# Products spread over four steps, latent heads in pairs, side steps after the third tile, and 768 tokens as 384 and 384

## The chip, the cores and the metric

The kernel runs on one core of a Trainium2 chip, as one launch. The metric is the time of the launch in microseconds on the device, as the median of several runs. TensorE (PE) multiplies; its weight loads (PEld) are told apart in the profile. VectorE (DVE), ScalarE (ACT) and GpSimd (POOL) do the element-wise work, SyncE (SP) starts most transfers. Lines such as L822 are lines of the kernel before.

## The reference

Two transformer blocks of two layers each are run one after the other on 512 tokens of 1024 features, all in float32. In layer 0 of the first block 256 context tokens run along, so that its linears see 768 tokens. Cut to what the change touches:

```python
# first block, layer 0 (with context): dense attention; layer 1: a band of 128 tokens plus the context, with a sink logit
p = jax.nn.softmax(s, axis=-1).astype(v.dtype)
o = jnp.einsum('bkgqt,btkd->bqkgd', p, v)
h = modulate(x, g_pre_mix[l], sh_m, sc_m); hc = modulate(ctx, g_pre_mix[l], csh_m, csc_m)
x = x + gt_f * rmsnorm(swiglu(h, w_ffn_in[l], w_ffn_out[l]), g_post_ffn[l])     # and the same for ctx in layer 0

# second block, layer 0: eight heads share one latent of 128 features and one rope key of 32
qc = jnp.concatenate([q_lat, q_rope], axis=-1)
kc = jnp.concatenate([c_kv, k_rope], axis=-1)
_, idx = lax.top_k(score, k_sel)                     # 128 tokens are kept of those up to the query
s = jnp.einsum('bqhc,bqkc->bqhk', qslice(qc, i, Q_BLOCK), kg).astype(jnp.float32) * A_SCALE
p = safe_softmax(s, valid)
return jnp.einsum('bqhk,bqkc->bqhc', p.astype(kg.dtype), kg[..., :A_KV_RANK])
```

## The kernel before

The features lie on the partitions and the tokens along the free axis. Each step of the network is a stage (a class derived from `Stage`); every engine has its own program, written out stage by stage, and the engines meet through semaphores. No scheduler moves anything: the order on each engine is that of the code.

**Linears** (`Linear`, the PE line L822, and L800 for the first two tiles of a linear whose input is still being made). A linear goes by output tiles of 128 features, called slabs. A slab's weights come in float32, ACT copies them to `w_hi` (L638), POOL subtracts to `w_lo` (L760), and PE multiplies hi by hi, hi by lo and lo by hi for each chunk of 128 input features. PE waits for `w_hi`, for `w_lo` before the last third, and for `psum_free`, the sign that DVE has emptied the two PSUM banks of the slab two before. The tokens are cut into groups, `self.groups`, and each group is a matmul with a weight load of its own. At 768 tokens the groups are 512 and 256 (258 where two columns of shift sums ride along). With `halves`, which only the shifted linears of 512 tokens have, they are 256 and 258. In the first block's layer 0 some linears also have `ModRows` beside them: DVE sums rows of the modulation weights (L389) in the same loop.

**Side steps** (`RopeBeside` and its children `WindowBeside`, `LatentBeside`, `CompressBeside`). While a linear runs, its finished tiles are rotated: PE multiplies a tile by a rotation matrix (L1095), POOL multiplies by the cosine (L1104), DVE does the sine and the sum (L1123, L1125). `beside.tensor(pe, m)` is called after slab m's matmuls and works on tile m - 1, for which it waits on `tile_out`. The first two slabs are done together by `two`, and steps 0 and 1 are called right behind it.

**Attention** (`Attend`). A unit is one head and 128 queries: scores on PE (L2499, the masks L2501), the row maximum on DVE (L1711), the exponential on ACT (L1768), the transposes of the probabilities on PE in two parts (L1666 into bank 4, L1671 into bank 5), copied out by DVE (L1742) and ACT (L1781). Four units are a batch with one output bank; B batches make a turn. `steps` sets one unit at each step and, Z + 1 steps later, part of the batch before. With `spread=True` (layer 0, its context, and the two window stages of layer 1) the batch's products are 4 that spread 1/sum over the columns (L2509) and 4 to 12 with the values (L2513), each onto 64 of the 128 output partitions; all of them are issued at the batch's step 0. ACT copies the spread columns at step 3 (L1795) and DVE multiplies at step 4 (L2520). The latent heads of the second block use `Attend` too, without `spread`: 16 batches of two units, J = 2.

`PairAttend` is the other form: two heads in one round, their scores in two PSUM banks, one `tensor_reduce` for both. The differential heads use it with `one` (the two heads are summed before the transposes) and the last attention without.

Of the kernel before, what the change touches and what calls it, by code (L numbers as in the profile page):

```python
# [522 lines left out]
class Linear(Stage):  # L523
# [7 lines left out]
    def __init__(self, kit, w, hi, lo, groups, mode, dst=None, segs=None, side=None, rows=None, norm=None, post=None, tiles=None, close=False, latent=()):  # L531
# [10 lines left out]
        self.halves = self.shifted and self.T == SEQ  # L542
        self.groups = [(0, SEQ // 2), (SEQ // 2, SEQ + 2)] if self.halves else ([(0, SEQ), (SEQ + 2, TOK + 4)] if norm.twice else [(0, SEQ), (SEQ, TOK + 2)]) if self.shifted else groups
# [23 lines left out]
    def main(self, s):  # L567

        k = self.kit
        return k.ps[:, 2 * s:2 * s + 2, 0:SEQ // 2] if self.halves else flat(k.ps[:, self.step * s:self.step * s + self.step])[:, :self.T]  # L570
# [9 lines left out]
    def shift_sums(self, s):  # L580
        return self.kit.ps[:, 2 * s + 1, SEQ // 2:SEQ // 2 + 2]
# [63 lines left out]
    def empty(self, eng, scale, m, e):  # L645
# [3 lines left out]
        tokens = self.tokens  # L649
        if self.norm:  # L650
            r = k.n_r[:, :T].unsqueeze(1)
# [5 lines left out]
            ins = eng.scalar_tensor_tensor(two(dst[:, 0, :]) if tokens is not self.tokens else dst, src, scale, r, ALU.mult, ALU.mult)  # L657
# [16 lines left out]
        if self.mode == "add":  # L674
            ins = eng.tensor_tensor(dst, src, dst, ALU.add)  # L675
        elif scale != 1.0:
            ins = eng.tensor_scalar(dst, src, scale, None, ALU.mult)
        else:
            ins = eng.tensor_copy(dst, src)
# [125 lines left out]
    def tensor(self, pe):  # L805
        k = self.kit

        def tile(m, i, e, parts=None, wait=lambda part, c: None):
# [35 lines left out]
        if isinstance(a, (Modulation, Gate)):  # L844
# [8 lines left out]
            if self.beside:  # L853
                for m in range(2):
                    self.beside.tensor(pe, m)
            self.slabs(pe, tile, 2)
            return
        if a and a.post:
# [10 lines left out]
            if self.beside:  # L869
                for m in range(2):  # L870
                    self.beside.tensor(pe, m)
            self.slabs(pe, tile, 2)
            return
        if a and a.mode == "gated":
# [6 lines left out]
            if self.beside:  # L881
                for m in range(2):
                    self.beside.tensor(pe, m)
# [648 lines left out]
class Attend(Stage):  # L1532
# [115 lines left out]
    def tensor(self, pe):  # L1648
# [32 lines left out]
        def output(j, n, i):  # L1681
# [120 lines left out]
class PairAttend(Stage):  # L1802
# [8 lines left out]
    def __init__(self, kit, J, scores, pv, prepare, finish, pt, one, adds=None):  # L1811
        super().__init__(kit)
        self.J, self.N, self.B, self.scores, self.pv, self.prepare, self.finish, self.pt, self.one, self.adds = J, J * QT, J * 2, scores, pv, prepare, finish, pt, one, adds
# [3 lines left out]
            ("pv_ready", self.B), ("spread_ready", 0 if one else self.B), ("o_free", self.B),  # L1817
# [28 lines left out]
    def tensor(self, pe):  # L1846
# [5 lines left out]
        def turn_round(p):  # L1852
            nt = p % QT + 1
            if self.one:
                pe.wait_ge(*self.count("prepared", p + 1))
                if p >= 2:
                    pe.wait_ge(*self.count("pt_b", p - 1))
# [7 lines left out]
        def output(b):  # L1865
            pe.wait_ge(*self.count("pt_b", 2 * b + 2))
            if not self.one:
                pe.wait_ge(*self.count("pt_a", 2 * b + 2))
                pe.wait_ge(*self.count("prepared", 2 * b + 2))
# [15 lines left out]
    def vector(self, dve, chain):  # L1885
# [6 lines left out]
        def take(b):  # L1892
            dve.wait_ge(*self.count("pv_ready" if self.one else "spread_ready", b + 1))
# [22 lines left out]
    def scalar(self, act, chain):  # L1916
# [15 lines left out]
        for p in range(self.N):  # L1932
            if p + 1 < self.N:
                exp(p + 1)
            if not self.one and p >= 3 and p % 2 == 1:
# [3 lines left out]
        if not self.one:  # L1939
# [517 lines left out]
def plan(k, d):  # L2457
# [172 lines left out]
    def scores_latent(pe, s, j, a, qi):  # L2630
        rows, n, q = slice(32 * a, 32 * a + 32), (qi + 1) * P, slice(qi * P, (qi + 1) * P)
        pe.matmul(s[:, 0:n], k.qlat[:, 4 * j + a, q], k.ckv_s[:, 0:n], start=True, stop=False, skip_group_check=True)  # L2632
# [318 lines left out]
```

## Time and profile before

| | |
|---|---|
| median of three runs | 3372.45 us (3364.27 to 3375.6) |
| the profiled execution | 3378.23 us, span 3376.4 us |
| mean granted TensorE clock | 0.943 |
| PE busy | 3076.1 us (91%), 16970 matmuls |
| DVE, ACT, POOL busy | 51%, 33%, 31% |
| HBM | 253.03 MB read, 76 GB/s over the span |

The page counts an engine as busy from an instruction's start to its end, and a matmul's end is modelled, so that two matmuls in a row overlap and a busy PE may still be waiting. What one matmul costs is read from starts: a row of the chain of waits gives the time of a run of matmuls and their number.

### The profile page before, as it was taken

How to read it: one execution, taken by the hardware profiler on the slowest of the kernel's cores; microseconds unless marked ns; L12 is line 12 of the kernel's file. 1: busy time of each engine (PE TensorE's matmuls, PEld its weight loads, DVE VectorE, ACT ScalarE, POOL GpSimd, SP SyncE). 2: the span in 40 equal slices, each digit the busy share in tenths (PEclk: the TensorE clock that was granted, in tenths of full speed). 3: DMA queues.
4: the chain of work that ended last, by engine and by line, in shares of the span. 5: the costliest groups of instructions: out<-in, count | busy, mean ns of one | idle time of the engine just before them, and what ended most of it. 6: DMA issues, size and time to landing. Idle time of an engine off the chain costs nothing.

```text
span 3376.4 us, 48629 instructions
## 1 busy us (share of the span) xinstructions
PE 3076.1 (91%) x16970; PEld 2493.5 (74%) x16970; DVE 1709.3 (51%) x2892; ACT 1101.2 (33%) x1904; POOL 1052.0 (31%) x573
## 2 busy tenths in 40 slices
PE   6778779999997888899998999899999999899997
PEld 3666668888886766699895765688887866688886
DVE  4755768864335566433245766342333247643433
ACT  3145143111124255432224324352223226552222
POOL 1121122323322311244443420244444301244443
PEclk8889989999998899899999988899999969999998
DMA  6200413434211100222222210222223100022222
GB/s 238 77 1 8 142 63 127 171 124 137 75 50 45 43 1 33 67 89 93 94 84 69 75 38 1 80 98 93 93 93 118 55 15 2 14 97 96 93 94 81
DMA packets 74344, 258.83 MB, mean 77 GB/s; under 512 B 9456, under 2 KB 12016, under 8 KB 72688
## 3 DMA queue, kind: packets, MB, share of 16 engines
q1 hardware_dynamic: 60256, 205.61, 18.4%
q10 hardware_dynamic: 13968, 51.65, 4.5%
q8 instruction: 73, 1.20, 0.1%
q14 instruction: 47, 0.39, 0.0%
HBM read 253.03 MB, written 2.10 MB: 76 GB/s over the span
## 4 chain that ended last, share of the span: by engine, by line
PE 81%; DVE 6%; issue 6%; ACT 3%; DVEq 1%; SPq 1%; ACTq 1%; POOL 0%; DMA 0%; POOLq 0%; PEldq 0%
PE ps L822 56%; PE ps L800 6%; PE ps L2513 2%; PE ps L2499 2%; PE ps L2656 1%; PE ps L426 1%; PE ps L1862 1%; PE ps L1095 1%; DVE ps L389 1%; PE ps L2720 1%; PE ps L1666 1%; DVE nm L1711 1%; ACT w_hi L638 1%; PE ps L2633 1%; PE ps L2632 1%
## 5 line engine op out<-in xcount | busy, mean ns | idle before, releaser
L760 POOL TENSOR_TENSOR w_lo<-w_raw,w_hi 128x1024 fp32r<-128x1024 f32 (+1 forms) x373 | 919.6, 2468 | 1823.5 <-ACT w_hi L638 1823.5
L638 ACT ACTIVATE w_hi<-w_raw 128x1024 fp32r<-128x1024 f32 (+1 forms) x373 | 385.6, 1038 | 1192.3 <-PE ps L822 948.0
L822 PE MATMUL ps<-h_hi,w_hi 128*128 128x258 f32 (+2 forms) x1824 | 315.6, 326 | 50.1 <-ACT w_hi L638 46.1
L822 PEld LDWEIGHTS ps<-h_hi,w_hi 128*128 128x128 f32 x1824 | 268.4, 195 | 85.6 <-issue 45.1
L822 PE MATMUL ps<-h_lo,w_hi 128*128 128x258 f32 (+2 forms) x1824 | 299.7, 316 | 0.0
L822 PE MATMUL ps<-h_hi,w_lo 128*128 128x258 f32 (+2 forms) x1824 | 296.7, 314 | 0.0
L822 PEld LDWEIGHTS ps<-h_lo,w_hi 128*128 128x128 f32 x1824 | 260.2, 190 | 24.4 <-DVE h_lo L2275 0.4
L822 PEld LDWEIGHTS ps<-h_hi,w_lo 128*128 128x128 f32 x1824 | 258.4, 189 | 23.1
L918 DVE CAST act_hi<-f_t 128x512 f32 (+1 forms) x88 | 165.8, 1884 | 12.6
L822 PE MATMUL ps<-hb_hi,w_hi 128*128 128x512 f32 x672 | 166.7, 390 | 2.0 <-issue 1.7
L822 PE MATMUL ps<-hb_hi,w_lo 128*128 128x512 f32 x672 | 166.0, 389 | 0.0
L822 PE MATMUL ps<-hb_lo,w_hi 128*128 128x512 f32 x672 | 166.0, 389 | 0.0
L822 PE MATMUL ps<-act_hi,w_hi 128*128 128x512 f32 (+1 forms) x660 | 151.6, 375 | 13.4 <-ACT w_hi L638 13.0
L822 PE MATMUL ps<-act_lo,w_hi 128*128 128x512 f32 (+1 forms) x660 | 149.4, 371 | 0.0
L822 PE MATMUL ps<-act_hi,w_lo 128*128 128x512 f32 (+1 forms) x660 | 148.6, 370 | 0.0
L822 PEld LDWEIGHTS ps<-hb_hi,w_hi 128*128 128x128 f32 x672 | 125.7, 188 | 30.4 <-issue 4.5
L822 PEld LDWEIGHTS ps<-hb_lo,w_hi 128*128 128x128 f32 x672 | 126.1, 188 | 26.2
L822 PEld LDWEIGHTS ps<-hb_hi,w_lo 128*128 128x128 f32 x672 | 126.1, 188 | 26.2
L1711 DVE TENSOR_REDUCE nm<-ps 128x1 f32<-128x512 f32 (+5 forms) x144 | 100.7, 700 | 88.2 <-PE ps L2501 45.7
L822 PEld LDWEIGHTS ps<-act_hi,w_hi 128*128 128x128 f32 x660 | 115.2, 190 | 40.7 <-issue 11.0
L675 DVE TENSOR_TENSOR x<-ps,x 128x512 f32 x64 | 44.3, 692 | 196.1 <-PE ps L822 166.1
L822 PE MATMUL ps<-ha_hi,w_hi 128*128 128x512 f32 x472 | 135.5, 431 | 8.9 <-ACT w_hi L638 7.9
(345 smaller groups left out, 5179.9 us busy)
## 6 DMA issues: line engine op xcount, KB each, us to landing
w_raw<-in_ffn_in SPq DMA_DIRECT2D x176, 512.0 KB, 3.4
mod_row<-in_w_mod_rows ACTq DMA_DIRECT2D x80, 512.0 KB, 4.3
w_raw<-in_ffn_out SPq DMA_DIRECT2D x64, 512.0 KB, 3.4
w_raw<-in_ev_in SPq DMA_DIRECT2D x26, 512.0 KB, 3.5
w_raw<-in_ffn_out SPq DMA_DIRECT2D x32, 384.0 KB, 3.0
w_raw<-in_od_in SPq DMA_DIRECT2D x21, 512.0 KB, 3.4
mod_ring<-in_w_mod SPq DMA_DIRECT2D x8, 1024.0 KB, 13.2
w_raw<-in_wo_in SPq DMA_DIRECT2D x12, 512.0 KB, 3.5
```

Of the source, the lines that this page charges most:

```text
L389: dve.scalar_tensor_tensor(flat(k.ps[:, 6:8]), k.mod_row[:, s, q], 1.0, (k.c_x, k.c_c)[j][:], ALU.mult, ALU.mult, accum_out=k.modv[:, tile ...
L426: ins = pe.matmul(k.ps[:, bank + g, 0:t1 - t0], k.ones[:], squares[:, t0:t1], start=start, stop=stop, skip_group_check=True)
L638: act.activation(k.w_hi[:, s, 0:self.KT * P], k.w_raw[:, s, 0:self.KT * P], ACT.Copy).then_inc(k.sems["w_hi_ready"], 1)
L675: ins = eng.tensor_tensor(dst, src, dst, ALU.add)
L760: ins = pool.tensor_tensor(k.w_lo[:, s, 0:self.KT * P], k.w_raw[:, s, 0:self.KT * P], k.w_hi[:, s, 0:self.KT * P].bitcast(F32), ALU.subtract)
L800: ins = pe.matmul(k.ps[:, self.step * s + g, 0:t1 - t0], w[:, s, c * P:(c + 1) * P], h[:, c, t0:t1], start=(e not in begun), stop=(left[e] ...
L822: ins = pe.matmul(k.ps[:, self.step * s + g, 0:t1 - t0], w[:, s, c * P:(c + 1) * P], h[:, c, t0:t1], start=(n == 0), stop=(n == len(parts) ...
L918: chain.mark(dve.tensor_copy(k.act_hi[:, at, :T], k.f_t[:, :T].unsqueeze(1)))
L1095: pe.matmul(self.bank(n), self.tiles[n].get("rot", self.rot), self.src(n), start=True, stop=True).then_inc(self.kit.sems["rot_mm"], 1)
L1711: ins = dve.tensor_reduce(k.nm[:, u % 4, 0:1], self.sc(u, n), AX.X, ALU.max, negate=True)
L2499: ins = pe.matmul(s[:, c:c + width], k.qs[:, a, q0:q0 + P], keys[:, part, t0:t0 + width], start=(part == 0), stop=(part == 1 and not masks ...
L2513: return made + [lambda i=i, a=a, slot=slot, t=t, c0=c0, c1=c1: pe.matmul(o[64 * a:64 * a + 64, c0:c1], v(a, t), pt[:, n % 2, a, slot, c0: ...
```

## The change

Four edits are made at once.

1. `Attend.output` loses its case for `spread`: a batch's products are issued in four parts at steps 0 to 3 (4, 4, 4, 4 in layer 0; 2, 2, 2, 2 for its context; 2, 4, 4, 4 in the windows), and `pv_ready` comes with the last part.
2. The latent heads go to `PairAttend`, two heads a round and 16 rounds in place of 32 units. `PairAttend` gets `spread` as an argument of its own, apart from `one`.
3. Side steps 0, 1 and 2 all follow slab 2.
4. `halves` also holds for linears of 768 tokens, except the one whose norm has `twice` (`wo_in`): groups 384 and 384, or 384 and 386 with the shift columns. These are `we_in`, `we_out`, and the six linears of the first feed-forward network.

```diff
+        self.half = self.T // 2
+        self.halves = self.shifted and self.T == SEQ or self.T == TOK and not (self.shifted and norm.twice)
+        self.groups = [(0, self.half), (self.half, self.T + 2 * self.shifted)] if self.halves else [(0, SEQ), (SEQ + 2, TOK + 4)] if self.shifted else groups
...
+        return k.ps[:, 2 * s:2 * s + 2, 0:self.half] if self.halves else flat(k.ps[:, self.step * s:self.step * s + self.step])[:, :self.T]
...
             if self.beside:
-                self.beside.tensor(pe, m)
+                for step in (range(3) if m == 2 else [m]):
+                    self.beside.tensor(pe, step)
...
             self.two(pe, order)
-            if self.beside:
-                for m in range(2):
-                    self.beside.tensor(pe, m)
             self.slabs(pe, tile, 2)
...
-            if self.spread:
-                part = lambda i: len(products) if i else 0
-            else:
-                part = lambda i: len(products) * i // self.Z // 2 * 2 if i < self.Z else len(products)
+            part = lambda i: len(products) * i // self.Z // 2 * 2 if i < self.Z else len(products)
             for product in products[part(i):part(i + 1)]:
                 ins = product()
-            if i == (0 if self.spread else self.Z - 1):
+            if i == self.Z - 1:
                 ins.then_inc(S["pv_ready"], 1)
...
+    turns2 = [(j, half) for j in range(2) for half in range(2)]
+
+    def scores_latent(pe, s, turn, qi):
+        j, half = turns2[turn]
+        n, q = (qi + 1) * P, slice(qi * P, (qi + 1) * P)
+        for a in range(2):
+            pe.matmul(s[:, a, :], k.qlat[:, 4 * j + 2 * half + a, q], k.ckv_s[:, 0:n], start=True, stop=False, skip_group_check=True)
+        for a in range(2):
+            at = 32 * (2 * half + a)
+            rows = slice(at, at + 32)
+            pe.matmul(s[:, a, :], k.qkv2[rows, 12 + j, q], k.qkv2[rows, 1, 0:n], start=False, stop=False, skip_group_check=True, tile_position=(at, 0))
+        for a in range(2):
+            ins = pe.matmul(s[:, a, :], k.ident_b, k.chosen[:, qi, 0:n], start=False, stop=True, skip_group_check=True)
+        return ins
+
+    def scaled(dve, chain, rinv, probs, turn, qi):
+        return dve.tensor_tensor(probs, probs, rinv.unsqueeze(2).to_broadcast([P, 2, (qi + 1) * P]), ALU.mult)
+
+    def latent_pv(pe, o, b):
+        both = o.rearrange("p (a q) -> p a q", a=2)
+        for i, (slot, t, c0, c1) in enumerate(causal_terms(b % 2)):
+            ins = pe.matmul(both[:, :, c0:c1], k.ckv_tok[:, t, :], k.pt_pair[:, b % 2, :, slot, c0:c1], start=(i == 0), stop=True, skip_group_check=True)
+        return ins
...
+    PairAttend(k, len(turns2), scores_latent, latent_pv, scaled, latent_out, k.pt_pair)
```

The order of instructions on PE in a window stage, from one batch's end to the next: `ps<-ident,rinv` are the spread products, `ps<-pt,v_tok` those with the values, `ps<-ident,probs` the transposes. Before:

```order
L2509 MATMUL ps<-ident,rinv 64x128 x4
L2513 MATMUL ps<-pt_78,v_tok 64x256 x8
L2513 MATMUL ps<-pt_78,v_tok 64x128 x2
L1569 UNCONDITIONAL_BRANCH
L1569 ISA
L2499 MATMUL ps<-keys_80,qs 128x512 x2
L2501 MATMUL ps<-masks 128x128
L1664 REGISTER_ALU
L1666 MATMUL ps<-ident,probs 128x128 x3
L1671 MATMUL ps<-ident,probs 128x128 x2
```

and now:

```order
L2503 MATMUL ps<-ident,rinv 64x128 x2
L1564 UNCONDITIONAL_BRANCH
L1564 ISA
L2493 MATMUL ps<-keys_80,qs 128x512 x2
L2495 MATMUL ps<-masks 128x128
L1659 REGISTER_ALU
L1661 MATMUL ps<-ident,probs 128x128 x3
L1666 MATMUL ps<-ident,probs 128x128 x2
L2503 MATMUL ps<-ident,rinv 64x128 x2
L2507 MATMUL ps<-pt_78,v_tok 64x256 x2
```

The 14 products stood together; now 2 stand at step 0, and each of the next units is followed by 4.

The start of the latent stage on PE: `ps<-ckv_s,qlat` is the latent part of a score, `ps<-qkv` the rope part on 32 rows, `ps<-chosen,masks` the mask. Before:

```order
L2632 MATMUL ps<-ckv_s,qlat 128x128
L2633 MATMUL ps<-qkv_75 128x128
L2634 MATMUL ps<-chosen,masks 128x128
L1666 MATMUL ps<-ident,probs 128x128
L2632 MATMUL ps<-ckv_s,qlat 128x256
L2633 MATMUL ps<-qkv_75 128x256
L2634 MATMUL ps<-chosen,masks 128x256
```

and now:

```order
L2631 MATMUL ps<-ckv_s,qlat 128x128 x2
L2635 MATMUL ps<-qkv_75 128x128 x2
L2637 MATMUL ps<-chosen,masks 128x128 x2
L1855 MATMUL ps<-ident,probs_82 128x128 x6
L2646 MATMUL ps<-pt_pair,ckv_tok 128x512
L2646 MATMUL ps<-pt_pair,ckv_tok 128x2x128
```

The same parts of two heads now stand side by side, and the products take both heads in one instruction.

The start of `wo_in` on PE, behind the first two slabs (`ps<-h_lo,w_hi`): `ps<-qkv,rot_a` is the rotation of the side step. Before:

```order
L800 MATMUL ps<-h_lo,w_hi 128x512
L800 MATMUL ps<-h_lo,w_hi 128x258
L1095 MATMUL ps<-qkv,rot_a 128x512
L822 MATMUL ps<-h_hi,w_hi 128x256
L822 MATMUL ps<-h_hi,w_hi 128x258
```

and now, with the end of slab 2:

```order
L825 MATMUL ps<-h_hi,w_lo 128x256
L825 MATMUL ps<-h_hi,w_lo 128x258
L1090 MATMUL ps<-qkv,rot_a 128x512 x2
L825 MATMUL ps<-h_hi,w_hi 128x256
L825 MATMUL ps<-h_hi,w_hi 128x258
```

The rotation of tile 0 stood ahead of slab 2; now it stands behind it, together with that of tile 1.

## Rows read from the trace of the kernel before

**Rows 1.** The page: the span, and busy time of each engine

```profile
span 3376.4 us, 48629 instructions
...
PE 3076.1 (91%) x16970; PEld 2493.5 (74%) x16970; DVE 1709.3 (51%) x2892; ACT 1101.2 (33%) x1904; POOL 1052.0 (31%) x573
```

**Rows 2.** Stretches: start:end, us, then PE, PEld, DVE, ACT, POOL busy, clock, DMA

```profile
1986.60:2007.00 20.40, 20.40 (x46) 9.57 (x46) 6.82 (x22) 4.18 (x15) 0.00 (x0) 0.50 0.01 1
...
596.00:675.00 79.00, 75.63 (x419) 63.84 (x418) 67.84 (x82) 8.47 (x8) 22.87 (x9) 1.00 0.51 173
...
2009.81:2019.14 9.33, 9.33 (x43) 5.52 (x42) 5.69 (x20) 3.08 (x12) 0.00 (x0) 1.00 0.00 1
1197.26:1206.04 8.78, 7.59 (x67) 5.96 (x67) 5.67 (x20) 5.17 (x18) 1.59 (x4) 1.00 0.00 0
...
304.08:308.68 4.60, 4.42 (x33) 2.88 (x33) 2.77 (x12) 2.87 (x13) 1.47 (x4) 1.00 0.00 0
```

**Rows 3.** PE's instructions in a window batch: start, us, what

```profile
1197.75 2.12 PE L2513 MATMUL ps<-pt,v_tok 128*64 128x256 f32 x20
1199.79 0.73 PE L2499 MATMUL ps<-keys,qs 128*128 128x512 f32 x2
...
1205.73 0.38 PE L1671 MATMUL ps<-ident,probs 128*128 128x128 f32 x2
1206.04 0.33 PE L2509 MATMUL ps<-ident,rinv 128*64 128x128 f32 x2
```

**Rows 4.** Whom PE waited for, 1179 to 1245: us in total, times, longest

```profile
PE ps L1666 <- DVE pt L1742: 8.7, 16, 1.2
```

**Rows 5.** The same from 224 to 292, in layer 0's attention

```profile
PE ps L1666 <- DVE pt L1742: 3.3, 8, 1.0
```

**Rows 6.** PE in the latent stage, a unit with 512 keys: start, us, what

```profile
2016.39 1.02 PE L2632 MATMUL ps<-ckv_s,qlat 128*128 128x512 f32 x2
...
2017.34 1.12 PE L2633 MATMUL ps<-qkv 32*128 32x512 f32 x2
2018.39 0.39 PE L2634 MATMUL ps<-chosen,masks 128*128 128x512 bf16 x1
2018.62 0.27 PE L1666 MATMUL ps<-ident,probs 128*128 128x128 f32 x1
```

**Rows 7.** PE in ev_in: two heads on 64 rows each, 128 to 512 keys

```profile
1846.62 2.75 PE L1355 MATMUL ps<-qkv 64*128 64x128 f32 x16
```

**Rows 8.** DVE groups, latent stage and a linear: times, us, mean ns, idle before

```profile
L2647 DVE TENSOR_SCALAR probs<-probs,rinv 128x512 f32<-128x512 f32 x1 | 0.5, 486 | 0.0
...
L920 DVE TENSOR_TENSOR act_lo<-f_t,act_hi 128x768 f32 x7 | 6.7, 959 | 0.9
```

**Rows 9.** The start of wo_in, then of ev_in: start, us, what [idle before]

```profile
1071.92 0.95 DVE L657 SCALAR_TENSOR_TENSOR qkv<-ps,n_r 128x768 f32<-128x768 f32 x1
...
1075.90 2.07 PE L1095 MATMUL ps<-qkv,rot_a 128*128 128x512 f32 x2 [6.69 <-DVE qkv L664]
...
1076.99 4.42 PE L822 MATMUL ps<-h_hi,w_hi 128*128 128x256 f32 x16
...
1817.69 1.13 PE L1095 MATMUL ps<-qkv,rot_b 128*128 128x512 f32 x2 [3.19 <-DVE qkv L657]
```

**Rows 10.** Runs of matmuls on the chain that ended last: start, us, what

```profile
675.06 126.04 PE ps L822 x720
...
818.73 51.14 PE ps L822 x288
...
1542.09 91.45 PE ps L822 x768
...
2205.84 76.47 PE ps L822 x336
```

**Rows 11.** PE, last attention, two heads on 64 rows each, 384 keys

```profile
2844.36 0.34 PE L2656 MATMUL ps<-lo,q_hi 64*128 64x384 f32 x2
2844.53 0.34 PE L2656 MATMUL ps<-qkv_hi,lo 64*128 64x384 f32 x2
```

More of the change, by code:

```diff
@@ L580, in shift_sums @@
     def shift_sums(self, s):
-        return self.kit.ps[:, 2 * s + 1, SEQ // 2:SEQ // 2 + 2]
+        at = self.half if self.halves else SEQ // 2
+        return self.kit.ps[:, 2 * s + 1, at:at + 2]
     def feed(self):
@@ L1802, with __init__ @@
 class PairAttend(Stage):
-    def __init__(self, kit, J, scores, pv, prepare, finish, pt, one, adds=None):
+    def __init__(self, kit, J, scores, pv, prepare, finish, pt, one=False, spread=False, adds=None):
         super().__init__(kit)
+        self.spread = spread
         self.J, self.N, self.B, self.scores, self.pv, self.prepare, self.finish, self.pt, self.one, self.adds = J, J * QT, J * 2, scores, pv, prepare, finish, pt, one, adds
@@ L1816, in __init__ @@
             ("tr_a", 0 if one else self.N), ("pt_a", 0 if one else self.N), ("tr_b", self.N), ("pt_b", self.N),
-            ("pv_ready", self.B), ("spread_ready", 0 if one else self.B), ("o_free", self.B),
+            ("pv_ready", self.B), ("spread_ready", self.B if spread else 0), ("o_free", self.B),
             ("part_ready", self.B if adds else 0), ("part_used", self.B if adds else 0))}
@@ L1853, in turn_round @@
             nt = p % QT + 1
-            if self.one:
+            if not self.spread:
                 pe.wait_ge(*self.count("prepared", p + 1))
-                if p >= 2:
-                    pe.wait_ge(*self.count("pt_b", p - 1))
+            if self.one and p >= 2:
+                pe.wait_ge(*self.count("pt_b", p - 1))
             for a in ((1,) if self.one else (0, 1)):
@@ L1892, in take @@
         def take(b):
-            dve.wait_ge(*self.count("pv_ready" if self.one else "spread_ready", b + 1))
+            dve.wait_ge(*self.count("spread_ready" if self.spread else "pv_ready", b + 1))
             if self.adds and b >= 2:
@@ L1934, in scalar @@
                 exp(p + 1)
-            if not self.one and p >= 3 and p % 2 == 1:
+            if self.spread and p >= 3 and p % 2 == 1:
                 spread((p - 3) // 2)
@@ L1938, in scalar @@
             act.activation(self.turned(p, 0 if self.one else 1), k.ps[:, self.bank(p, 1), 0:(p % QT + 1) * P].rearrange("p (t c) -> p t c", c=P), ACT.Copy).then_inc(S["pt_b"], 1)
-        if not self.one:
+        if self.spread:
             spread(self.B - 1)
@@ L2636, in whole_pv @@
-    def whole_pv(v, head):
-        def pv(pe, o, j, n):
-            return [lambda i=i, slot=slot, t=t, c0=c0, c1=c1: pe.matmul(
-                o[:, c0:c1], v(j, t), k.pt4[:, n % 2, head(n), slot, c0:c1], start=(i == 0), stop=True, skip_group_check=True)
-                for i, (slot, t, c0, c1) in enumerate(causal_terms(n % 2))]
-        return pv
-    Attend(k, 2, [[(n // 2, 2 * (n % 2) + i, i, True) for i in range(2)] for n in range(8)], scores_latent,
-           causal_tiles, lambda n, qi: 0, whole_pv(lambda j, t: k.ckv_tok[:, t, :], lambda n: n // 2 % 2),
-           lambda dve, chain, j, u, a, qi, probs, rinv: dve.tensor_scalar(probs, probs, rinv, None, ALU.mult), no_marks,
-           lambda dve, chain, o, j, n: dve.tensor_copy(k.qkv2[:, 4 + 4 * j + n // 2, 256 * (n % 2):256 * (n % 2) + 256], o[:, 0:256]), k.pt4)
+    turns2 = [(j, half) for j in range(2) for half in range(2)]
@@ L2729, in plan @@
     PairAttend(k, len(turns3), scores3, pv3, gated, lambda dve, o, b: dve.tensor_tensor(k.parts[:, b % 2, :], o[:, 0:256], k.spread[:], ALU.mult),
[L2730 removed]
+               k.pt_pair, spread=True, adds=add_part)
     Split(k, [(k.o_t[:, m, :], *in_ha(m)) for m in range(8)], chunks=range(8))
```

32 lines of the change are left out of this document (11 added, 21 removed).

## The prediction

> **What bounds the kernel now.** I read the page first [rows 1]: PE is busy for 91% of the span, no other engine for more than 51%. So a term counts where PE gets less to do, or waits less. What one matmul costs I took from the chain of waits, whose rows give the time and the number of matmuls of a run in which PE never waited [rows 10]; then the stretches of the stages that the change touches [rows 2], and in each the list of whom PE waited for [rows 4, 5]. In the windows PE waits for DVE's copy of transposed probabilities, in the latent stage for nobody, in the 768-token linears for nobody except where DVE sums modulation rows.
>
> **The sum's base.** The durations are of one execution, which took 3378.23 us (span 3376.4). The median of the runs is 3372.45, 5.8 lower; I subtract the sum from the median. Three runs lie between 3364 and 3376, so 0.3%, 10 us, is about what a measurement can tell from no change.
>
> **Edit 1, products in four parts.** What it adds: a product works on 64 of the 128 output columns of the array, its neighbours on all. The row shows that such a switch costs: the 20 instructions from 1197.75 run two by two, 8 pairs of 256 columns and 2 of 128, and the next starts 2.04 later; at 4 cycles a column for both halves of a float32 product (0.216 and 0.109 a pair) that is 1.94, so 0.10 goes at the exit. On the way in, two transposes of 0.109 take 0.31 until the product starts, 0.09 more [rows 3]. A batch has one way in and out now and four after: +0.6 us a batch, and there are 28 batches (16 window, 8 in layer 0, 4 of its context), +16.8 us if nothing is won.
>
> What it removes: in the windows PE waits 8.7 us in 16 waits over 66 us, that is 7.2 batches of 9.1, so 1.2 a batch [rows 4]; the modelled ends hide about 0.3 more of late starts. These waits stand at the units without products behind them: a unit is 1.15 to 1.3 us of PE work, but DVE needs some 1.9 from a unit's last score to the copied transposes (maximum 0.69, sink 0.3, sum and reciprocal 0.35, copy 0.56). With 0.86 + 0.2 of products behind a unit PE takes 2.0 to 2.2 and is late itself. Only step 0, with two products, stays near 1.6 and keeps about 0.3 of wait. So of 1.5 us all but 0.3 go, 0.6 come: -0.6 a batch, and -0.7 with the batch's end, which no longer holds up the next maximum; 16 batches, -11 us. Bounds: waits of 1.5 all gone at no further price, 16 x 0.9 = -14; waits untouched, +10. I take the row of waits.
> In layer 0 the waits are 3.3 us over 7 batches, 0.5 each, and late starts as much again [rows 5]: 0.9 - 0.6 = -0.3, less for step 0, so I take -0.2 x 8 = -1.5 us (bounds -3, +4). The context batch takes 4.6 us for 3.4 of PE work [rows 2]: half of the wait may go, -0.25 x 4 = -1 us (bounds -2, +2). ACT now really waits for `pv_ready` at step 3; behind that wait stand its copy of the next unit's transposes, which PE makes 1.4 us later, and the spread copy of 0.39, so there is room. DVE's multiply at step 4 comes a little later and frees a bank that is next wanted four steps on. Edit 1: -13.5 us.
>
> **Edit 2, latent heads in pairs.** A latent head takes 9.33 us and PE is busy throughout [rows 2]. At 512 keys the latent part takes 0.95, the rope part 1.05, the mask 0.23 [rows 6]; 512 columns at 4 cycles are 0.85, so 0.1 goes on entering the 32-row form and 0.2 on leaving it. Paired, two things shrink. The changes of form are made once for two heads: 4 x 0.3 = 1.2 us per two heads. And the two rope parts lie on different rows and in different PSUM banks. Two heads on 64 rows each, float32, 128 to 512 keys, took 2.75 us for 16 instructions [rows 7]; one after the other 2 x 1280 columns would be 4.27. So they ran side by side, and I expect it of 32 rows too: one of the two rope parts is free, 1280 columns or 2.13 us per two heads. PE's work falls from 18.66 to 15.3 us per two heads.
> The Trainium skill (TensorEngine Tiling (Array Packing), Key Properties) says that tiles execute in parallel and that four of 32 x 128 exist; no run here shows 32 rows. By that rule the 2.13 go, without it they stay.
> What is late next: a DVE that takes whole rounds. At the round of 384 keys PE's own queue holds only the next turn's 128-key scores (1.1 us), while DVE still has the 512-key maximum of two heads (1.2), a copy (0.4), the output copy (0.7), then reciprocal and scaling (1.2). I count 1.8 us of wait for PE there, so a turn of two heads takes 17.2, -1.5 us x 4 = -6, of which the longer run-out of the last pair gives back 1: -5 us. Half of the first two heads is done at half clock (20.4 us at 0.50, rows 2), which scales both. Bounds: no wait, -13; rope parts one by one, +3.
> The Trainium skill (VectorE: DVE Perf Modes, Mode 2×_2P) has a rule against this edit: float32 `tensor_scalar` gets two results a cycle from SBUF, `tensor_tensor` one, and the scaling goes from the first to the second. The rows agree: 512 elements took 486 ns as tensor_scalar, 768 took 959 as tensor_tensor [rows 8]. By the rule 1024 take 1.25, scaled from the old row 0.97; in the wait above this is 0.3 us a turn, 1 us in all.
>
> **Edit 3, side steps after slab 2.** In `wo_in` PE stood idle 6.69 us until 1075.90, for DVE's addition to tile 0, then rotated (1.09 to the next start), then began slab 2 at 1076.99 [rows 9]. Slab 2 itself needs bank 0 empty, which DVE's evacuation gives at 1071.92 + 0.95, and a `w_hi` that is ready by 1073. So slab 2 starts 3.9 us earlier; the rotation then stands behind it, at 0.45: -3.5 us. What queues behind: DVE's sine for tile 0 now waits until slab 2 is done, and the evacuation of slab 2 behind it comes 1.5 us later; slab 4 wants that bank only a slab (5.7 us) later. In `ev_in` the rotation at 1817.69 was covered by a `w_hi` that came at 1818.1, so there the 0.45 is added. In `od_in` PE has no wait there: 0. Edit 3: -3 us (bounds -8, if the half clock that follows the idle time goes too, and +2).
>
> **Edit 4, 384 and 384.** The columns stay the same; only what a matmul costs beyond its columns can change. Per pair of groups: 512 + 258 take 350.1 ns (126.04 / 720 x 2), 29 over the 321 of 770 columns at 2.4 GHz. 512 + 256 take 355.1 (51.14 / 288 x 2), 35 over. 256 + 258 take 238.2 (91.45 / 768 x 2), 24 over; 512 after 512 takes 227.6 (76.47 / 336), 14 over, 28 a pair [rows 10]. So equal lengths cost 24 to 28 a pair, unequal ones 29 to 35. One nearer row speaks against: matmuls of 384 columns on half arrays follow each other at 170 to 176 ns [rows 11], 10 to 16 over, 32 a pair at worst. I take 27: -2 ns for the pairs with shift columns, -8 for the others. Bound by PE are about 1100 of the former (44 slabs of the gate linears, 6 of `we_in`, 24 pairs each) and 336 of the latter (the second and third down projection): -2.2 and -2.7, -5 us. Bounds: 32 over, +2.3; 24 over, -9. `we_out` and the first down projection win nothing: DVE is busy 67.84 of 79 us there with the rows' sums and sets the pace [rows 2]. DVE's reads in two pieces of 384 should cost as now.
>
> **Sum.** -13.5 - 5 - 3 - 5 = -26.5 us; from the profiled 3378.2 that gives 3351.7, from the median 3346.
>
> **Rivals.**
> - The waits come back. DVE's 1.9 us chain runs on its own clock: were PE made to wait at every step as now, edit 1 would cost 16.8 instead of giving 13.5: 3346 + 30 = 3376, no change. For it: the wait is for a bank that only DVE frees. Against: with products behind a unit PE takes longer than the chain, and today, where they are, no wait follows.
> - The packing doesn't pay: the 32-row rope parts run one by one (+8) and 384 costs 32 over (+7): 3361; either alone 3353. For it: no row has 32 rows side by side, and rows 11.
> - Slower: PE idles in pieces and the clock is taken back. The latent stage starts with 20.4 us at 1.2 GHz [rows 2]. A wait of 1.8 us in each turn of pairs, where now there is none, could hold the clock at its lower level through the stage; PE's 40 us of work in the rest of it would take 80: 3346 + 40 = 3386. It decides from some 30 us more at half clock. Against: the windows, with waits of 1.2 in each batch, ran at full clock.
> - More than forecast: idle time shrinks at `wo_in`, and the 10 us at half clock behind it are spared, as are some of the latent stage's: -5 and -7, 3334.
>
> **Chances.** The forecast 0.60 (own range 3336 to 3358), packing doesn't pay 0.15 (3352 to 3364), waits come back 0.08, clock lost 0.07, clock won 0.10. Faster than 3362.3: nearly all of the first, 0.8 of the second, the last: 0.81. Slower than 3382.6: 0.07 and a rest of the waits, 0.09. Between: 0.10. The range from 3330 to 3365 leaves out the waits, the lost clock and a little at the lower end, together 0.2.
>
> **What would show it.** In the changed kernel: a window batch of 8.4 us in place of 9.1, PE's waits for L1742's copy under 0.5 a batch; a latent turn of two heads of 17 us, its two rope parts starting within 10 ns of each other, and PE waiting once a turn for DVE's scaling; PE idle 4 us instead of 6.7 at the start of `wo_in`; runs of 384 and 386 at 173 to 175 ns a matmul. I am wrong if the batch stays at 9.1, if the rope parts follow each other at 0.43, or if PE's clock stands at half for longer than before.

## The result and the profile after

The changed kernel took 3349.16 us (median of five, 3346.5 to 3350.15) where the kernel before took 3372.45; the ratio of the two is 0.9932, 95% interval 0.9919 to 0.9945, so 0.7% faster. Forecast were 3346 and 3330 to 3365. The profiled execution has a span of 3348.4 us, 28.0 less than before; the medians differ by 23.3. The profiled execution of the kernel before was a long one: a second one had a span of 3366.7 (below).

The page after, against [rows 1]:

```profile
span 3348.4 us, 48380 instructions
...
PE 3062.7 (91%) x16922; PEld 2558.0 (76%) x16922; DVE 1705.9 (51%) x2820; ACT 1104.2 (33%) x1896; POOL 1049.8 (31%) x573
```

What bounds the kernel is the same. The stages, in microseconds from a stage's first matmul to the first of the next, in two profiled executions of each kernel (the second ones, "again", are among the experiments). Slabs are counted from 0. The row of the windows begins in the middle of the last slab of `wo_in`, the row of the last attention with the last slab of the linear ahead of it.

| stage | before | again | after | again | forecast |
|---|---|---|---|---|---|
| first linear to `we_out` (layer 0's attention, its context) | 286.2 | 286.3 | 284.9 | 285.0 | -2.5 |
| first feed-forward network | 601.4 | 600.3 | 596.6 | 596.8 | -5 |
| `wo_in`, up to its slab 3 | 46.5 | 45.0 | 41.6 | 41.6 | -3.5 |
| window attentions | 183.5 | 182.9 | 174.1 | 174.1 | -11 |
| `ev_in`, up to its slab 4 | 36.9 | 36.9 | 38.3 | 38.3 | +0.45 |
| latent heads | 86.6 | 86.6 | 77.8 | 77.8 | -5 |
| differential heads | 75.0 | 69.4 | 72.7 | 72.7 | 0 |
| last attention | 224.2 | 224.2 | 223.7 | 224.5 | 0 |

**Windows.** A batch at full clock takes 8.7 us on average, from the scores of a unit to those of the same unit a batch later, where it took 9.1. First PE's instructions in such a batch, with start, us and what; then the list of whom PE waited for in the first of the two window stages, 1156 to 1225 (us in total, times, longest), as [rows 4] has it of before.

```profile
1189.93 1.08 PE L2507 MATMUL ps<-pt,v_tok 128*64 128x256 f32 x8
1190.95 0.73 PE L2493 MATMUL ps<-keys,qs 128*128 128x256 f32 x4
...
1192.12 0.87 PE L2507 MATMUL ps<-pt,v_tok 128*64 128x256 f32 x8
...
1194.34 0.44 PE L2503 MATMUL ps<-ident,rinv 128*64 128x128 f32 x4
...
1196.59 0.60 PE L2507 MATMUL ps<-pt,v_tok 128*64 128x256 f32 x4
...
1198.63 1.08 PE L2507 MATMUL ps<-pt,v_tok 128*64 128x256 f32 x8
1199.65 0.72 PE L2493 MATMUL ps<-keys,qs 128*128 128x512 f32 x2
```

```profile
PE ps L1661 <- DVE pt L1734: 1.2, 3, 0.6
PE ps L2493 <- ACT sink_exp L1763: 1.1, 1, 1.1
```

Each unit now has products behind it. The waits for DVE's copy fell from 8.7 us in 16, over 66 us, to 1.2 in 3, over 69.

**Latent heads.** The start of the round of 512 keys in the first, second, third and fourth turn of two heads, with the first turn's wait:

```profile
1975.61 1.88 PE L2631 MATMUL ps<-ckv_s,qlat 128*128 128x512 f32 x4
...
1981.80 0.87 PE L1855 MATMUL ps<-ident,probs 128*128 128x128 f32 x6 [1.19 <-DVE probs L2641]
...
1992.29 1.88 PE L2631 MATMUL ps<-ckv_s,qlat 128*128 128x512 f32 x4
...
2011.20 1.88 PE L2631 MATMUL ps<-ckv_s,qlat 128*128 128x512 f32 x4
...
2028.48 1.88 PE L2631 MATMUL ps<-ckv_s,qlat 128*128 128x512 f32 x4
```

PE at the third turn's round of 512 keys, against [rows 6]; the next round's scores of 128 keys; and the wait of that turn:

```profile
2013.01 1.13 PE L2635 MATMUL ps<-qkv 32*128 32x512 f32 x4
2014.07 0.60 PE L2637 MATMUL ps<-chosen,masks 128*128 128x512 bf16 x2
2014.52 0.60 PE L1855 MATMUL ps<-ident,probs 128*128 128x128 f32 x4
2014.95 0.61 PE L2631 MATMUL ps<-ckv_s,qlat 128*128 128x128 f32 x4
...
2015.91 0.28 PE L2637 MATMUL ps<-chosen,masks 128*128 128x128 bf16 x2
2017.99 0.87 PE L1855 MATMUL ps<-ident,probs 128*128 128x128 f32 x6 [1.79 <-DVE probs L2641]
```

Four rope matmuls (two heads) take 1.06 us from their start to the mask's, as long as two took before; those of the two heads start 7 ns apart. In the first turn PE waits 1.19 us for DVE's scaling, and the next turn begins 16.68 us later. In the second and third it waits 1.79, the 1.8 of the forecast, since DVE now has an output copy of 0.68 to make as well; the third, all of it at full clock, takes 17.28 (the second has 3.4 us at half clock in it). Two heads took 18.66 before.

**Linears.** The runs of matmuls on the chain that ended last, against [rows 10]: start, us, what.

```profile
672.69 126.44 PE ps L825 x720
...
816.49 50.20 PE ps L825 x288
867.12 101.21 PE ps L825 x576
```

A pair of 384 and 386 costs 351.2 ns (126.44 / 360) where 512 and 258 cost 350.1: slower. A pair of 384 and 384 costs 348.6 (50.20 / 144) where 512 and 256 cost 355.1.

**Side steps.** The starts of `wo_in` and `ev_in`, against [rows 9]:

```profile
1067.03 2.56 PE L825 MATMUL ps<-h_hi,w_hi 128*128 128x256 f32 x16 [3.85 <-ACT w_hi L640]
...
1074.34 1.88 PE L1090 MATMUL ps<-qkv,rot_a 128*128 128x512 f32 x4
...
1798.42 3.35 PE L825 MATMUL ps<-ha_hi,w_hi 128*128 128x512 f32 x8 [3.57 <-ACT w_hi L640]
...
1805.60 1.02 PE L1090 MATMUL ps<-qkv,rot_b 128*128 128x512 f32 x2
```

PE idles 3.85 us in `wo_in` instead of 6.69 and a rotation, and now for `w_hi`. In `ev_in` slab 2 waits for `w_hi` as it did, so the rotation behind it is added.

### The profile page after: what moved, and what is told of

The parts are those of the page before. It is cut to its first block, busy times and chain, and to the rows that moved or that the text cites. A ratio compares the mean times of both kernels' runs of the same rounds, so it can differ in the third digit from the quotient of the medians.

```text
span 3348.4 us, 48380 instructions
## 1 busy us (share of the span) xinstructions
PE 3062.7 (91%) x16922; PEld 2558.0 (76%) x16922; DVE 1705.9 (51%) x2820; ACT 1104.2 (33%) x1896; POOL 1049.8 (31%) x573
## 3 DMA queue, kind: packets, MB, share of 16 engines
q1 hardware_dynamic: 60256, 205.61, 18.9%
## 4 chain that ended last, share of the span: by engine, by line
PE 84%; DVE 5%; issue 5%; ACT 3%; DVEq 1%; SPq 1%; POOL 1%; ACTq 0%; DMA 0%; POOLq 0%; PEldq 0%
PE ps L825 58%; PE ps L803 6%; PE ps L2493 2%; PE ps L2507 2%; PE ps L1855 1%; PE ps L426 1%; PE ps L2661 1%; PE ps L1090 1%; PE ps L1661 1%; PE ps L2725 1%; ACT w_hi L640 1%; DVE ps L389 1%; PE ps L1666 1%; DVE nm L1884 1%; PE ps L2031 1%
## 5 line engine op out<-in xcount | busy, mean ns | idle before, releaser
L825 PE MATMUL ps<-h_hi,w_hi 128*128 128x384 f32 (+4 forms) x1824 | 314.4, 326 | 54.5 <-ACT w_hi L640 50.1
L825 PEld LDWEIGHTS ps<-h_hi,w_hi 128*128 128x128 f32 x1824 | 289.3, 194 | 69.0 <-issue 45.9
L825 PE MATMUL ps<-h_hi,w_lo 128*128 128x384 f32 (+4 forms) x1824 | 298.9, 316 | 0.0
L825 PE MATMUL ps<-h_lo,w_hi 128*128 128x384 f32 (+4 forms) x1824 | 298.3, 316 | 0.0
L825 PEld LDWEIGHTS ps<-h_hi,w_lo 128*128 128x128 f32 x1824 | 280.9, 189 | 3.8
L825 PEld LDWEIGHTS ps<-h_lo,w_hi 128*128 128x128 f32 x1824 | 280.3, 190 | 3.5
L908 DVE TENSOR_TENSOR f_t<-ps,n_r 128x512 f32<-128x512 f32 x44 | 30.4, 691 | 202.1 <-PE ps L825 198.4
```

Source lines behind the costliest of these rows:

```text
L825: ins = pe.matmul(k.ps[:, self.step * s + g, 0:t1 - t0], w[:, s, c * P:(c + 1) * P], h[:, c, t0:t1], start=(n == 0), stop=(n == len(parts) ...
```

## The experiments

"Before" in a ratio is the kernel before, run on the same chip.

**Each edit alone.** The kernel before with one edit of the diff.

only1: edit 1.

```diff
-            if self.spread:
-                part = lambda i: len(products) if i else 0
-            else:
-                part = lambda i: len(products) * i // self.Z // 2 * 2 if i < self.Z else len(products)
+            part = lambda i: len(products) * i // self.Z // 2 * 2 if i < self.Z else len(products)
...
-            if i == (0 if self.spread else self.Z - 1):
+            if i == self.Z - 1:
```

> Edit 1 alone (products in four parts). Theory from the two traces: 16 window batches at 8.7 us instead of 9.1 and shorter hand-overs between the stages, together about -9; layer 0 and its context together about -1.5; so 10 to 11 us faster than before, 3362. Rival, that part of the 9 belongs to the clock (the changed kernel has 3.4 us less at half clock in the windows): 7 to 8 us. The rival of the prediction (waits come back) would be 0 or slower; the trace of the changed kernel speaks against it.

Measured: 3357.8, ratio 0.9964 (0.9951 to 0.9976), which is 12 us faster, 8 to 17. In the trace the windows win 9.5 us (9.0 against the second profile of before) and the way up to `we_out` 1.9. So the waits did go, and did not come back. The first feed-forward network, whose code edit 1 doesn't touch, takes 596.8 us here, as in the changed kernel; the part on the prediction comes back to it.

only2: edit 2.

```diff
-    Attend(k, 2, [[(n // 2, 2 * (n % 2) + i, i, True) for i in range(2)] for n in range(8)], scores_latent,
...
+    PairAttend(k, len(turns2), scores_latent, latent_pv, scaled, latent_out, k.pt_pair)
```

> Edit 2 alone (latent heads in pairs). Theory, work and waits only: the latent stage took 77.7 us instead of 86.5, and 3.4 us of this is the half clock (6.8 us less of it at half), so 5 to 6 us faster than before. Rival, the shorter stretch at half clock is a result of the edit (the waits of 1.8 us come later, the stage starts with its short rounds) and comes back here: 8.7 faster, and with the differential heads behind it, which also had 7 us less at half clock, 11.

Measured: 3357.8, ratio 0.9959 (0.9946 to 0.9971), 14 us faster, 10 to 18. The latent stage took 77.6 us, with the same 13.7 at half clock as in the changed kernel, so 9 come from there; the differential heads took 68.3 where before took 75.0 and 69.4, and in this profile the last attention was 8.7 shorter. That profile's execution, 3352.5 us, was among the fastest of the kernel's twelve. The rival (the clock's share goes with the edit) is nearer than the theory of 5 to 6.

only3: edit 3.

```diff
-                self.beside.tensor(pe, m)
+                for step in (range(3) if m == 2 else [m]):
+                    self.beside.tensor(pe, step)
...
             self.two(pe, order)
-            if self.beside:
-                for m in range(2):
-                    self.beside.tensor(pe, m)
             self.slabs(pe, tile, 2)
```

> Edit 3 alone (side steps after slab 2). Theory: -4.2 us in wo_in (slab 2 starts 3.9 earlier), +2 in ev_in (three rotations stand between slab 2 and 3 that were hidden before), 0 in od_in: 2 us faster, not to be told from no change. Rival, the clock decides both places: anything from -5 to +2, with half-clock stretches at other places than in the changed kernel.

Measured: 3372.4, ratio 0.9993 (0.9975 to 1.001): no change can be told. In the trace slab 2 of `wo_in` starts 3.9 us earlier, and `wo_in` up to slab 3 takes 44.0 against 45.0 to 46.5 in the two profiles of before. `ev_in` takes 38.9 against 36.9: 0.45 are the rotation's, the rest a stretch at half clock (3.4 us from 1814.6) which before did not have there.

only4: edit 4.

```diff
+        self.half = self.T // 2
+        self.halves = self.shifted and self.T == SEQ or self.T == TOK and not (self.shifted and norm.twice)
+        self.groups = [(0, self.half), (self.half, self.T + 2 * self.shifted)] if self.halves else [(0, SEQ), (SEQ + 2, TOK + 4)] if self.shifted else groups
```

> Edit 4 alone (384 and 384). Theory: pairs of 384 + 386 cost 1.1 ns more than 512 + 258 (351.2 against 350.1), +1.2 us over 44 slabs of 24; the third and second down projection win 6.7 ns a pair, -2.1; the start of the first gate linear wins 1.4; together 2 to 3 us faster, hardly to be told from no change. Rival, my prediction's term, 5 us faster.

Measured: 3373.3, ratio 1.0002 (0.999 to 1.0014): nothing, and my 5 us are outside the interval. The chain of only4 has the changed kernel's durations. That of only1, whose linears are as before, has those of before, but for the third down projection. First two rows of only4 (the second down projection, x288, and the third gate linear), then two of only1 (the second gate linear and the second down projection):

```profile
817.56 50.21 PE ps L825 x288
868.21 101.22 PE ps L825 x576
```

```profile
672.60 126.04 PE ps L822 x720
815.97 51.14 PE ps L822 x288
```

The third down projection, from 985 to 1021 or from 994 in the kernel before, is one row of the chain in each: of before, of only1, and of the changed kernel.

```profile
993.99 27.20 PE ps L822 x154
```

```profile
984.98 36.07 PE ps L822 x208
```

```profile
984.89 36.07 PE ps L825 x208
```

Before took 353 ns a pair there, but only1 took 346.8 with the same groups of 512 and 256, and so did the changed kernel with 384 and 384. The pairs of 512 and 256 run at one of two paces; by starts 353.3 or 346.7. The pace changes between executions too: before_again ran the third projection at 353.3 as well, but the second at 346.7, and its row of the chain is shorter than the 51.14 us of [rows 10]:

```profile
817.56 50.19 PE ps L822 x288
```

Where the faster one holds anyway, edit 4 wins nothing.

**e12: edits 1 and 2 together** (both diffs above).

> Edits 1 and 2 without 3 and 4. Theory: edits 3 and 4 gain nothing, so this is as fast as the changed kernel, 3349 (within 3). The two gains measured apart (0.9964 and 0.9959) would make 3346 if they simply add. Rival: edits 3 and 4 win their 5 us only in company of the others (other places of the half-clock stretches), then this kernel is at 3354.

Measured: 3348.0, ratio 0.993 (0.9915 to 0.9946), the changed kernel's time. The theory holds: edits 3 and 4 are worth nothing that can be told. In the traces edit 3 wins 3.5 us in `wo_in` against this kernel (45.1 to 41.6) and gives 0.6 back in `ev_in`; the first feed-forward network takes 597.1 us without edit 4 and 596.6 with it. What hides this in the time are stages whose code is the same in both: above all the latent heads, 75.0 us here with 6.8 at half clock, against 77.8 with 13.7.

**rope_one_block: the rope parts of a pair on the same rows.**

```diff
-            at = 32 * (2 * half + a)
+            at = 32 * (2 * half)
```

> The changed kernel, but the rope parts of both heads of a pair use the same 32 rows of the array (the second head reads the first one's rope rows, so the scores differ from the reference). If the two rope parts ran side by side in the changed kernel, a round of 512 keys shows 2.0 to 2.1 us from rope start to mask where it was 1.06, and the latent stage is 1280 columns or 2.1 us longer in each of 4 turns at most, 6 to 8.5 us in all (part of it falls into the wait of 1.8 us at the 128-key round): 3356. Rival, that the gain of pairing came from fewer changes of form alone: no change, and both rounds alike.

Measured: 3350.6, ratio 0.994, of a kernel whose second head of each pair takes the rope part of the first. The latent stage took 86.2 us instead of 77.8, with 13.7 at half clock in both: +8.4, the upper end of the theory. PE's row at the round of 512 keys:

```profile
2014.62 1.88 PE L2631 MATMUL ps<-ckv_s,qlat 128*128 128x512 f32 x4
2016.42 1.98 PE L2635 MATMUL ps<-qkv 32*128 32x512 f32 x4
2018.56 0.38 PE L2637 MATMUL ps<-chosen,masks 128*128 128x512 bf16 x1 [0.16 <-issue]
```

The same four matmuls take 2.14 until the mask, where they took 1.06. That parts on different rows, in different banks, run side by side is thereby shown. The time as a whole missed the forecast of 3356: the next stage, the differential heads, took 67.5 us instead of 72.7, with 15.6 at half clock instead of 33.0.

**two_scalars: the scaling of a pair as two instructions.**

```diff
-        return dve.tensor_tensor(probs, probs, rinv.unsqueeze(2).to_broadcast([P, 2, (qi + 1) * P]), ALU.mult)
+        for a in range(2):
+            ins = dve.tensor_scalar(probs[:, a], probs[:, a], rinv[:, a:a + 1], None, ALU.mult)
+        return ins
```

> The changed kernel with the scaling of a pair as two tensor_scalar in place of one broadcast tensor_tensor. At 384 keys the one took 0.96 us; 384 elements as tensor_scalar took 0.42 in the kernel before, so two take 0.8. Theory: PE's wait in each turn (7.7 us in 4 waits) shrinks by 0.15 to 0.3 a turn, about 1 us in all, 3348, not to be told by the time but by the waits. Rival: PE waits for the maximum before it, not for the scaling, and the waits stay at 7.7.

Measured: 3342.5, ratio 0.9912 (0.9895 to 0.9928). DVE's two instructions for 384 keys, and PE's wait behind them:

```profile
2009.12 0.75 DVE L2642 TENSOR_SCALAR probs<-probs,rinv 128x384 f32<-128x384 f32 x2
...
2009.93 0.87 PE L1855 MATMUL ps<-ident,probs 128*128 128x128 f32 x6 [1.58 <-DVE probs L2642]
```

0.75 instead of 0.96, and the wait is 1.58 instead of 1.79: the scaling is the end of what PE waits for. The first turn takes 16.47 us instead of 16.68, so 0.2 less. That is the 1 us of the theory. The rest is clock: the latent stage took 72.5 us with 3.4 at half clock instead of 77.8 with 13.7, and the differential heads 67.4 instead of 72.7. The profile is of the fastest of five executions, 3334.4 us, so these two differences are larger than that of the medians, 6.7.

**two_parts: the products of a batch in two parts.**

```diff
-            part = lambda i: len(products) * i // self.Z // 2 * 2 if i < self.Z else len(products)
+            part = lambda i: (len(products) // 4 * 2 if i < 3 else len(products)) if i else 0
...
-            if i == self.Z - 1:
+            if i == 2:
```

> The changed kernel with the products of a batch in two parts (steps 0 and 2) in place of four. Theory of the prediction (0.2 a change of form, and a unit without products behind it makes PE wait for DVE's chain): a window batch saves two pairs of changes, 0.4, and gets back the waits of steps 1 and 3, 0.3 to 0.5 each: 8.8 to 9.0 us where four parts took 8.7 and one part 9.1, PE's waits for the copies 0.6 to 0.9 a batch, 3350 to 3354. Rival, the changes of form are what is left and the waits belong to step 0 alone: 8.3 us a batch, 3343. In layer 0, where no batch got shorter by four parts, the first makes 9.7 to 9.8.

Measured: 3364.2, ratio 0.9983 (0.9969 to 0.9997), 15 us slower than four parts; the windows take 185.6 us instead of 174.1. The batches take 9.25 and 9.65 in turn, more than with one part (9.1 on average), and outside what either theory said (8.3, or 8.8 to 9.0). Whom PE waited for in five batches of the same stage (1180.6 to 1227.6):

```profile
PE ps L1661 <- DVE pt L1734: 6.6, 10, 0.9
```

Two waits a batch, 1.3 us. My theory had the sign and the places (the units of steps 1 and 3) but priced them too low: the waits are back as a whole, and the two changes of form saved don't pay for them. Against one part, two parts wait 0.1 us longer a batch and have one way in and out more (0.19 by the prediction); the batch is 0.33 us longer. In layer 0 a batch took 10.1 where four parts took 9.86 and one 9.77.

**best1: edit 3 in `wo_in` alone, edit 4 in the down projections alone.**

```diff
-        self.halves = self.shifted and self.T == SEQ or self.T == TOK and not (self.shifted and norm.twice)
+        self.halves = self.shifted and self.T == SEQ or self.T == TOK and not self.shifted
...
-        self.beside = beside
+        self.beside, self.late = beside, isinstance(beside, WindowBeside)
...
-                for step in (range(3) if m == 2 else [m]):
+                for step in (range(3) if m == 2 and self.late else [m]):
...
+            if self.beside and not self.late:
+                for m in range(2):
+                    self.beside.tensor(pe, m)
```

> The changed kernel with edit 3 in wo_in alone (ev_in and od_in as before) and edit 4 in the down projections alone (the shifted linears at 512 and 258 again). Theory: ev_in gets back 0.45 for sure and 1.8 where a half-clock stretch goes with it, the shifted linears 1.4 ns on each of 1200 pairs, 1.6: 2 to 4 us faster than the changed kernel, 3346. Rival: ev_in's 2.2 us were the clock's chance and stay; then 3347 to 3349, not to be told from it.

Measured: 3346.7, ratio 0.9922 (0.9904 to 0.994), and that can't be told from the changed kernel. In the trace `ev_in` gets back 0.45 and the shifted linears of the first network 1.0, but the third down projection took 67.0 instead of 65.4, with a stretch at half clock (3.4 us from 981.4) that the changed kernel doesn't have.

**before_again and after_again.** No edit.

> The kernel before, unchanged, a second profiled execution. It tells what belongs to an execution: the stage of the differential heads took 75 us with 41 us at half clock in three profiles and 67 us with 15 in four, of kernels whose code for it is the same. If the clock's stretches are set by the program (its waits), this profile shows 75 again and 58 us at half clock in the last attention; if by chance, 67 or another value there.

> The changed kernel, unchanged, a second profiled execution, for the same question: the differential heads' stage took 72.7 us with 33 us at half clock, the latent heads' 77.7 with 13.7. By the program: the same again; by chance: 67 to 75, and 72.5 to 77.7 (the range that other kernels with the same pairs showed).

Measured: 3368.2 and 3349.0. The stages are in the table above. The kernel before had the differential heads at 69.4 this time, not 75.0, with the same latent stage ahead. Their stretches in the two profiles (start:end, us, busy of PE, PEld, DVE, ACT and POOL, clock, DMA):

```profile
2072.30:2147.30 75.00, 56.69 (x296) 42.72 (x296) 39.77 (x98) 32.24 (x93) 0.00 (x0) 0.73 0.04 11
```

```profile
2068.10:2137.50 69.40, 50.65 (x297) 37.22 (x297) 39.72 (x98) 32.27 (x93) 0.00 (x0) 0.82 0.04 13
```

The first is the execution of [rows 2], the second before_again. The work is the same (DVE 39.77 and 39.72), the clock 0.73 and 0.82. So that stage's clock belongs partly to the execution. The changed kernel repeated itself to 0.2 us in the table, but for the last attention's 0.8.

**best2: best1 with the scaling of two_scalars.** Both diffs above.

> The changed kernel with edit 3 in wo_in alone, edit 4 in the down projections alone, and the scaling of a pair as two tensor_scalar. Theory: 1 us from the wait of each turn, 1 to 2 us from the linears, so 3346 by work and waits; the version with the two tensor_scalar alone came to 3342.5, of which the traces put 1 us down to the wait and the rest to the clock. If that clock goes with the shorter waits, this is 3341; if it was chance, 3346.

Measured: 3337.7 (3335.5 to 3340.0), ratio 0.9905 (0.9884 to 0.9926): faster than both kernels, all five runs below all nine of the changed kernel. The latent stage and the one of the differential heads in its profile:

```profile
1967.90:2040.80 72.90, 63.76 (x286) 35.63 (x290) 36.70 (x88) 24.43 (x80) 0.00 (x0) 0.98 0.00 1
2040.80:2108.20 67.40, 46.81 (x297) 34.57 (x297) 39.54 (x98) 32.39 (x93) 0.00 (x0) 0.88 0.04 12
```

Against the changed kernel that is -4.9 and -5.3 us, and these are its whole gain (3338.3 against 3348.4). By work and waits it should be 1 there; the rest is the clock. That the shorter waits bring this clock is not shown: with the long ones two_parts had as little half clock in the latent stage (3.4 us), and rope_one_block and only1 had the short stage of the differential heads (67.5 and 67.4).

## Why the prediction was right

The time and range held, 3 us from the forecast. Part of that is luck: one term was not there, others were smaller than forecast, and stages that the forecast left alone won by their clock. By its steps:

- **Edit 1, windows (-11).** Right in mechanism, too large. The stage won 9.4 and 8.8 us. The waits fell to 0.2 a batch or less, as said, but the batch came to 8.7 and not 8.4: 0.43 less than 9.12. The 1.2 of waits less 0.2, against 0.57 for three more ways in and out, make -0.4; the 0.3 of late starts that I had added to the waits didn't come back as time. 16 batches are 6.9 us, and 2 to 2.5 us came at the starts and ends of the two stages. two_parts shows the rule behind it from the other side: without products behind them the units of steps 1 and 3 make PE wait again.
- **Edit 1, layer 0 and its context (-1.5 and -1).** 1.3 were won, half of the forecast, and the step was wrong: a batch there got 0.09 longer (9.77 to 9.86), not 0.2 shorter. PE shows no wait from 224 to 292 any more, where [rows 5] had 3.3 us, that is 0.47 a batch, and the 0.57 of the changes of form took all of that. What won is the ends: the first two batches took 17.7 to 18.2 us instead of 19.0 to 19.1, the last one up to the context's first scores 19.6 to 19.7 instead of 20.0, and the context up to `we_out` 0.5 to 0.8 less.
- **Edit 2 (-5).** The wait was priced right, 1.79 for 1.8, and its place too; the turn of 17.2 came to 17.28. PE's work in a turn is 15.5 us (17.28 - 1.79, or 16.68 - 1.19 in the first), a little over my 15.3. The stage won 8.8 us, but not all by this. It had 13.7 us at half clock where before had 20.5. What those 6.8 us are worth, two_parts tells, whose latent stage has the same code: it took 74.1 us with only 3.4 at half. In the changed kernel the turn with 3.4 us at half clock took 18.9, 1.6 more than the 17.28, so half clock costs about half of its length. By that the stage of two_parts is some 72.4 us at full clock, and that of before, where PE was busy throughout the half clock, 76.3 (both are estimates). So at full clock the edit wins some 4 us, for a forecast of 5, and some 4.8 of the 8.8 are clock. The packing was a rule of the Trainium skill (TensorEngine Tiling (Array Packing), Key Properties: tiles execute in parallel) with no row for 32 rows; rope_one_block now gives one, 1.06 against 2.14 us, 8.4 us in all. The rule against the edit (the Trainium skill, VectorE: DVE Perf Modes, Mode 2×_2P: two results a cycle for float32 `tensor_scalar`, one for `tensor_tensor`) agrees as well: 768 elements took 0.96 in one `tensor_tensor` and 0.75 in two `tensor_scalar`, and PE's wait followed by 0.2.
- **Edit 3 (-3).** The 3.9 us at slab 2 of `wo_in` and the 0.45 in `ev_in` are in the traces to the tenth. The stages hold some clock besides: in `wo_in` 3.4 to 4.9 won, in `ev_in` 1.4 lost, of which some 0.9 come with edit 1 (only1, whose side steps are as before, has 37.9 there against 36.9). Alone the edit can't be told from nothing.
- **Edit 4 (-5).** This term was wrong, and it is the one that failed: it measured 0 (-3.4 to +4.7). Of the two prices one had the wrong sign: I took 27 ns over the columns for equal groups, -2 ns a pair with shift columns, from an interval of 24 to 32; it was +1.0 to +1.1, so some 30 over, towards the 32 of [rows 11], which I had weighed too low. (The pairs are 50 slabs of 24, 1200 and not 1100; that is 0.2 us.) The down projections' 8 ns were 6.6, and only where 512 and 256 run at their slower pace, which is a matter of the execution. The first network did get 3.5 to 4.8 us shorter, as much as forecast, but not by this: only1, without edit 4, has 596.8 us there. What shortened it is, by only1, other places of the half-clock stretches (1.6 us at one slab of the third projection, 1.4 at the start) and that pace. This goes with edit 1: the eight profiles of kernels with products in four parts have 596.6 to 597.2 us there with 13 to 20 at half clock, the six without, two_parts and only4 among them, 599.7 to 601.4 with 25 to 27. Why the attention ahead moves the clock's stretches there is not shown. Those 3 us are part of the 12 that only1 won, and nothing in my sum for edit 1 stands for them.
- **Rivals.** The waits did not come back; of "packing doesn't pay" the half about 384 came true in part, 30 over where it had 32; the clock was not taken back by the waits of the latent stage, it was won there: 13.7 us at half against 20.5. That part of the last rival is in the result.

So the sum, -26.5 forecast and -23.3 measured, came out near by terms that make up for each other. By work and waits I count some -18 from the stages: -9 in the windows, -1.3 in layer 0, -4 in the latent heads, -3.5 by edit 3, nothing by edit 4 (an estimate). The other 5 are clock that the sum had put at nothing: some 5 and 3 us won in the latent heads and in the first feed-forward network, the rest lost in other stages. The terms measured apart say the same: edit 2 alone was 14 us faster (10 to 18), where the forecast gave it 5.

What is open: what sets the clock in the latent stage and behind it. The same code had 3.4 to 13.7 us at half clock in the first and 15.5 to 42 in the second, some of it fixed by the kernel (after and after_again agree), some not (before and before_again don't).

## What to carry to other kernels

Where PE waits for a short chain on another engine after each unit, spread the work that is independent of the chain so that each unit has some behind it; half the places filled was no gain here, since the unfilled units waited as before and the changes of form came on top. Count those changes against the waits first: where the waits were 0.5 us a batch (layer 0), a batch got no shorter. Small matmul blocks on different row groups and in different banks are worth pairing, but look what the slower broadcast form does to the engine that PE then waits for. And where a stage's clock varies by more than an edit is worth, judge the edit by its stage in the trace, beside a second profile of the same kernel, and look at the stages behind it whose code is the same: an edit can win or lose time there too.

## What the runs showed of the hardware

- Alternating matmuls of 512 and 256 columns with a weight load each run at one of two paces, 353.3 or 346.7 ns a pair by starts, in the same loop of one program in two executions; 384 and 384 took 346.7 each time. 384 and 386 took 1.0 to 1.1 ns a pair more than 512 and 258.
- Four matmuls of 32 rows by 512 columns on two blocks of rows, into two banks, took 1.06 us; on one block 2.14.
- In one program the stage of the differential heads took 75.0 us at a granted clock of 0.73 and 69.4 at 0.82. The last attention begins with 51 to 58 us at half clock in all profiles but one (only2), which had 31 there and took 8.7 us less.
